# Prompt attention with pre-split operands, dilated sets scored by residue, and shares applied to the outputs

## The reference

```
def fox_prompt(q, k, v, logf):            # causal, with a learned decay
    c = cumsum(logf)
    s = q @ k.T * scale + c[query] - c[key]
    p = softmax(where(key <= query, s, -inf))
    return p @ v

def dilated_prompt(q, k, v, window, dilation):
    # tokens by residue modulo the dilation, then a causal band of window // dilation
    o, lse = band_attn(to_res(q), to_res(k), to_res(v), window // dilation)

for (w, r) in ((128, 1), (512, 4), (2048, 16)):   # each with q, k, v of its own
    o, lse = dilated_prompt(q, k, v, w, r)
a = softmax([lse_1, lse_2, lse_3])                 # merge_groups
o_dil = sum(a_g * o_g)                             # = one softmax over all three key sets
```

## Time and profile before

| | us |
|---|---|
| median of 3 runs (1779.42 to 1780.15) | 1779.7 |
| span of the profiled execution | 1779.2 |
| PE busy in it | 1710.8 |
| DVE busy | 1086.7 |
| ACT busy | 956.5 |
| POOL busy | 868.4 |
| prompt attention, from the first DMA of its block to the first matmul of the next | 1070.2 to 1256.0 |

### The profile page before, as it was taken

One profiled execution on the slowest core, in us unless ns is written; L12 is line 12 of the kernel. 1 busy time (PEld: TensorE's weight loads), 2 busy tenths in 40 slices (PEclk: granted clock), 3 DMA queues, 4 the chain that ended last, 5 costly groups with the idle time before them and its releaser, 6 DMA issues. The chain is left out here.

```text
span 1779.2 us, 32332 instructions
## 1 busy us (share of the span) xinstructions
PE 1710.8 (96%) x10749; PEld 1529.3 (86%) x10749; DVE 1086.7 (61%) x2480; ACT 956.5 (54%) x1649; POOL 868.4 (49%) x496
## 2 busy tenths in 40 slices
PE   6999999999889999999999977898999999999998
PEld 5888888899889999899899956888998989899897
DVE  6747556422388888888888877888444514234251
ACT  5444344432368887888888877988314313122230
POOL 1615233300338878778788747775233433333332
PEclk9999999999999999999999998999999999999999
DMA  7386585645889999999999976320645566666662
GB/s 238 106 290 216 202 300 183 207 132 137 253 308 365 344 351 350 353 347 336 355 360 349 316 232 163 91 73 25 215 146 214 235 259 236 259 236 260 236 259 77
DMA packets 191563, 427.76 MB, mean 240 GB/s; under 512 B 22761, under 2 KB 86122, under 8 KB 190002
## 3 DMA queue, kind: packets, MB, share of 16 engines
q1 hardware_dynamic: 187474, 415.29, 66.8%
q10 hardware_dynamic: 2560, 8.39, 1.6%
q0 software_dynamic: 1376, 2.10, 0.5%
HBM read 392.36 MB, written 120.64 MB: 288 GB/s over the span
## 5 line engine op out<-in xcount | busy, mean ns | idle before, releaser
L1086 POOL TENSOR_TENSOR vv_lo<-v_raw,vv_hi 128x1024 fp32r<-128x1024 f32 x178 | 401.4, 2261 | 147.9 <-ACT vv_hi L1175 145.7
L1986 POOL TENSOR_TENSOR w_lo<-w_raw,w_hi 128x2048 fp32r<-128x2048 f32 x39 | 180.1, 4619 | 318.4 <-ACT w_hi L2000 318.4
L1167 ACT ACTIVATE kt_hi<-ktp 128x1024 fp32r<-128x1024 f32 (+1 forms) x192 | 186.2, 970 | 94.0 <-PE ktp L1351 93.2
L1191 DVE TENSOR_TENSOR kt_lo<-ktp,kt_hi 128x1024 fp32r<-128x1024 f32 (+1 forms) x192 | 220.9, 1151 | 8.1 <-ACT kt_hi L1167 6.2
L1365 PE MATMUL s_ps<-kt_hi,q_st 128*128 128x256 f32 (+3 forms) x768 | 205.9, 302 | 0.8 <-DVE mx_parts L1241 0.4
L1351 PE MATMUL ktp<-ident,k_raw 128*128 128x128 f32 x1440 | 192.0, 276 | 8.3 <-DVEq L1182 3.8
L1351 PEld LDWEIGHTS ktp<-ident,k_raw 128*128 128x128 f32 x1440 | 168.6, 142 | 32.7 <-issue 5.6
L707 PE MATMUL acc<-w_hi,xn_hi 128*128 128x512 f32 x480 | 192.4, 401 | 2.4 <-POOL w_lo L340 2.4
L1175 ACT ACTIVATE vv_hi<-v_raw 128x1024 fp32r<-128x1024 f32 (+1 forms) x192 | 191.4, 997 | 6.2 <-PE o_ps L1381 5.7
L1365 PE MATMUL s_ps<-kt_lo,q_st 128*128 128x256 f32 (+3 forms) x768 | 191.0, 282 | 0.0
L707 PE MATMUL acc<-w_lo,xn_hi 128*128 128x512 f32 x480 | 187.7, 391 | 0.0
(11 more groups left out here) (244 smaller groups left out, 4139.4 us busy)
## 6 DMA issues: line engine op xcount, KB each, us to landing
k_raw<-in_cache_fox_k SPq DMA_DIRECT2D x256, 256.0 KB, 4.9
v_raw<-in_cache_fox_v SPq DMA_DIRECT2D x256, 256.0 KB, 4.6
out_win_kv_sample<-in_cache_win_kv SPq DMA_DIRECT2D x32, 2040.0 KB, 9.5
w_raw<-in_w_in SPq DMA_DIRECT2D x32, 1024.0 KB, 5.9
k_raw<-in_cache_win_kv SPq DMA_DIRECT2D x40, 512.0 KB, 9.5
v_raw<-in_cache_win_kv SPq DMA_DIRECT2D x40, 512.0 KB, 8.6
w_raw<-in_w_up SPq DMA_DIRECT2D x16, 1024.0 KB, 5.3
w_raw<-in_w_down SPq DMA_DIRECT2D x16, 1024.0 KB, 5.1
```

What stands on the lines that cost most here:

```text
L1086: gp.tensor_tensor(vv_lo[:, slot, 0:tiles, :], v_raw[:, i % RAW_RING, 0:tiles, :], vv_hi[:, slot, 0:tiles, :].bitcast(F32), ALU.subtract). ...
L1167: act.activation(kt_hi[:, slot, :, 0:n], ktp[:, i % 2, :, 0:n], ACT.Copy).then_inc(k_hi, 1)
L1191: ve.tensor_tensor(kt_lo[:, slot, :, 0:n], ktp[:, i % 2, :, 0:n], kt_hi[:, slot, :, 0:n].bitcast(F32), ALU.subtract).then_inc(k_lo, 1)
L1986: gp.tensor_tensor(w_lo[slot][:], w_raw[:, slot, :], w_hi[slot][:].bitcast(F32), ALU.subtract).then_inc(slab_lo_done, 1)
```

## The change

It does six things.

1. In `project_tokens` DVE makes the low parts of turned q and k (`turned_rows_lo`, 8 a set) and of v (4 a set), and ACT a high part of v (4 a set) beside the copy. High and low are stored whole, three stores a chunk, to `qh_s`, `ql_s`, `kh_s`, `kl_s`, `vh_s`, `vl_s`. The loops over sets on ACT and DVE become two loops, for sets 0 and 1, and for sets 2 and 3, whose turned columns are laid by residue modulo 4.
2. `attend_prompt` no longer splits anything. POOL issues the loads of the split operands, 2 for a pair's keys, 2 for a head's queries, 8 for a pair's values. Those of the first pair (with two of zeros, in place of `memset`) are issued inside `attend_sample`, after its last keys are scored (`first_pair`); SP issues masks and bias there.
3. Sets 2 and 3 are scored per residue modulo 4: 4 units of two tiles a head (`SPREAD`), which replace 20 tiles. Set 1 (`NEAR`, 7 tiles) and set 0 (`FAR`, 10 tiles) stay. A head has 25 tiles in 7 steps, with three output banks.
4. Each unit of each kind has its own minimum of the negated scores and its own sum: 12 exponentials a head. Probabilities are not normalised.
5. The shares that scale the outputs are worked out per head: NEAR's minima and sums go through DRAM to the residue layout (SP, `send_near`, `take_near`), DVE, POOL and ACT compute shares with small operations, SP stores them and `far`'s inverses and loads all three by broadcast (`send_far`, `send_shares`, `take_shares`).
6. POOL scales and adds the outputs of each pair (`scale`, 4 operations of 128x512). Outputs are evicted by ACT (`copy_spread`) and DVE (`copy_near`, `copy_far`).

```diff
@@ project_tokens, scalar and vector @@
+                if t == Q_TILES:
+                    act.activation(y_t[:, t, :], tp[:, slot, :], ACT.Copy).then_inc(yt_done, 1)
+                else:
+                    act.activation(token_cols(y_hi, t, by_residue), turned_cols(tp[:, slot, :], by_residue), ACT.Copy).then_inc(yt_done, 1)
+                            if t < Q_TILES:
+                                act.activation(v_hi[:, t, :], acc[:, t, :], ACT.Copy).then_inc(vhi_done, 1)
+            def turned_rows_lo(s, c, t, by_residue):
+                slot, at = (5 * c + t) % 2, 10 * s + 5 * c + t
+                ve.wait_ge(yt_done, at + 3)
+                ve.tensor_tensor(token_cols(y_lo, t, by_residue), turned_cols(tp[:, slot, :], by_residue),
+                                 token_cols(y_hi, t, by_residue).bitcast(F32), ALU.subtract).then_inc(ylo_done, 1)
@@ attend_sample, gpsimd @@
+            def first_pair(b, i):
+                if b < DEC_BATCH - 1 or i < LAST:
+                    return
+                done(gp, s_done, group_index(b, LAST))
+                hold(gp)
+                load_keys_of(gp, a, ahead, 0)
+                load_queries(gp, a, ahead, 0, 0)
+                gp.dma_start(ahead["q"][64:128, :, 0].rearrange("p c s n -> p c (s n)"), a["c_zero"].bitcast(F32R)).then_inc(ahead["zeroed"], 16)
...
+            straight(DEC_BATCH, PER_BATCH, (0, per_batch), (EXP_BEHIND, values_lo), (5, first_pair))
@@ attend_prompt @@
+SPREAD, NEAR, FAR = 0, 1, 2
+GROUPS = ((SPREAD, (0, 1)), (SPREAD, (2, 3)), (NEAR, (2, 3)), (NEAR, (0, 1)), (FAR, (3,)), (FAR, (2,)), (FAR, (0, 1)))
+S_BANKS, T_BANKS = 3, 2
@@ sync @@
+            def send_near(h, i):
+                if i == 0:
+                    sp.wait_ge(exp_done, STEPS * h + 4)
+                    sp.dma_start(a["stat_s"][h].rearrange("c (q p) -> p (c q)", p=P), stat[:, h % 2, NEAR].rearrange("p c q -> p (c q)"), allow_slow_non_contiguous=True).then_inc(near_sent, 16)
...
+            straight(HEADS, STEPS, (6, send_near), (7, take_near), (8, bias_ahead),
+                     (10, send_far), (12, send_shares), (13, take_shares))
@@ gpsimd @@
+            load_values(0)
+            gp.wait_ge(masks_in, 16)
...
+            straight(HEADS, STEPS, (0, mask_diagonals), (0, keys_ahead), (7, queries_ahead), (7, values_ahead), (9, gaps), (10, weights), (11, divide), (15, scale))
@@ scalar @@
+            straight(HEADS, STEPS, (EXP_P_BEHIND, exponentials), (TURN_BEHIND, turns_hi), (10, gap_exponentials), (10, copy_spread),
+                     (TURN_BEHIND + 1, split_lead))
@@ vector @@
+            def least_of_both(h, i):
+                if i == 0:
+                    ve.wait_ge(near_in, 16 * (h + 1))
...
+            straight(HEADS, STEPS, (KEEP_BEHIND, keep), (LOW_BEHIND, turns_lo), (9, invert_far), (9, least_of_both), (11, invert_whole), (12, copy_near), (14, copy_far))
             ve.wait_ge(lead_w, 1)
             ve.tensor_tensor(w0_lo[:], w_raw[:, 0], w0_hi[:].bitcast(F32), ALU.subtract)
@@ tensor: score @@
+                    if kind == SPREAD:
+                        lots = [(s, slice(n * P, (n + 1) * P), slice(cols.start + j * P, cols.start + (j + 1) * P)) for j, (s, _) in enumerate(unit_tiles(kind, n))]
+                    else:
+                        s = 0 if kind == FAR else 1
+                        lots = [(s, slice(unit_tiles(kind, n)[0][1] * P, (n + 1) * P), cols)]
+                    for s, keys, out in lots:
+                        for m, (q, part) in enumerate(((q_hi, 0), (q_lo, 0), (q_hi, 1))):
+                            last = pe.matmul(s_ps[:, at % S_BANKS, out], q[:, h % 2, s, n * P:(n + 1) * P], k[p % 2][:, part, s, keys], start=(m == 0), stop=(m == 2))
```

More of the change, by code:

```diff
@@ new lines, in mask_diagonals @@
+            def mask_diagonals(h, i):
+                if i:
+                    return
+                tiles = bias[:, h % 2, :].rearrange("p (t n) -> p t n", n=P)
+                causal = masks[:, 0:P].unsqueeze(1).to_broadcast([P, 2, P])
+                gp.wait_ge(bias_in[h % 2], 16 * (h // 2 + 1))
+                for part in (slice(0, 3, 2), slice(5, 10, 4)):
+                    last = gp.tensor_tensor(tiles[:, part], tiles[:, part], causal, ALU.add)
+                last.then_inc(diag_done, 1)
```

823 lines of the change are left out of this document (421 added, 402 removed).

## The result

The changed kernel takes 1875.3 us, median of 4 runs (1868.6 to 1883.1), against 1779.9 for the kernel before on the same chip: ratio 1.054 (95% interval 1.051 to 1.057). It is slower, and the prediction, 1767 and at most 1797, was wrong. The profiled execution is the longest of the four: its span is 1881.2 us, 102.0 over that of before, where the medians differ by 95.4.

A forecast was written before the change was run, and what follows sets the result against it. PE was taken to bound the prompt loop. Stage 136 + 8.5 + 3 + 15 = 162.5 against 185.8 (-23.3), projection +1.5, end of decode +6, clock +3: -12.8, forecast 1767 us, range 1742 to 1797.

The forecast's parts named there:

- The round trip of NEAR's numbers: Prompt loop: NEAR's exchange through DRAM takes 9 us, and four steps and one bank allow 12 before DVE needs it.
- The rival: Prompt loop: if NEAR's trip takes 15 us, every head loses 3 and the time is 1791; chance 0.07.
- The loop's traffic: Prompt loop: no cost was given to its loads; the DMA share of 0.26 was read from the kernel before.
- The loop, PE: Prompt loop: PE bounds it at 17.0 us a head, 136 for eight, -34.6, with 1.8 a head kept idle.
- The end of decode: End of decode: 5.6 MB more to fetch push back value loads or first scores, +6 us (0 to 18).
- The projection: Projection: DVE's low parts partly fall into its waits, +1.5 us (0 to 11); larger stores stay hidden.
- POOL's issues at 1.0 us: End of decode and prompt stage: each POOL load issue costs 1.0 us, between 0.6 and 4.0; eight take 8 us.
- that rival: Prompt loop and decode: POOL's issues make ACT wait, deciding at about 1.3 us each; 1814 at 2 us; chance 0.17.
- The 18 us by the rule on the shared port: End of decode: eight POOL issues, each waiting for a DVE split of up to 2.3 us, take 18; sum 1777.
- The ends of the stage: Prompt stage: start losses 8.5 us, pipeline drain 3, exposed exchange of the last head 15 (7 to 20).
- The next stage's clock: Last stage: PE idles before it and begins it at the lower clock, +3 us (0 to 7).
- The lower end of the range: Whole kernel: 1742 us, the cheap ends (1752) with half of the loop's idle time gone.

The follow-up runs named there:

- the probes: Kernel before, with SP in the prompt stage storing 4 KB and loading it back, in 4-byte then 32-byte pieces, four times each; 1792.3 us (single run).
- the run with later users: Changed kernel with minimum of both, gaps, weights, division and scaling five steps later and a third statistics buffer; 1876.0 us, ratio 1.052 to the kernel before.
- the run with local numbers and low parts once: Changed kernel without NEAR's trip through DRAM, low parts of q fetched for the first pair only, of k and v for the first two; 1807.2 us.
- the run with small bias: Changed kernel with 32-byte NEAR stores, vn ahead, memset zeros, v's stores behind slabs, later exchange users, and bias fetched as 4 tiles, not 10; 1799.0 us.
- the run with the 32-byte store: Changed kernel storing NEAR's numbers in 32-byte pieces and fetching them by four loads in 4-byte pieces; 1834.1 us, ratio 1.030 to the kernel before.
- vn first: Changed kernel with POOL's first-pair loads issued 12 steps later, behind the two vn loads; 1862.2 us, ratio 1.046 to the kernel before.
- loads early: Changed kernel with 32-byte NEAR stores, memset zeros, v's stores behind slabs, later exchange users, first-pair loads 11 steps earlier than in vn first; 1825.5 us.

## Why the prediction was wrong

- **The round trip of NEAR's numbers (9 us, 12 allowed): the step that failed first.** The store was priced at 5 from a transfer of 512 pieces of 256 bytes, bounds 2.8 and 10; in the probes it takes 10.2 to 12.1 at a DMA share of 0.30 to 0.50, above its own upper bound. The nearest row had pieces 64 times as long, and it was a load where the term is a store. The load was priced at 3 and takes 9.0 beside the loop's traffic (1.6 to 2.6 in the probes, in 32-byte rows). The rival had the mechanism and too small a price: its 1791 at 15 us a trip adds 24 us, and taking the trip away gave back 53, 5.8 us a head at trips of 18 to 25. The sentence beside it, one descriptor for each element, was the rule that spoke against the change, and its chance of 0.07 was too low for a transfer that no row showed. It also left out SP's list: by the run with later users the trip costs the same when DVE doesn't wait for it.
- **The loop's traffic: the step that was missing.** I costed the bytes of the extra loads in the projection and at the end of decode and not in the loop, and took the share of 0.26 of the kernel before for the one after. The loop's share became 1.18; a third of the operands' traffic is worth 2.0 to 2.7 us a head. The stage before moved some 15 MB; it is now 30.
- **The loop, PE (17.0 a head): not what bound it, and met in sum when it was.** With the trip gone and a third of the operands left out it measures 17.0, and the stage 164.7 against 162.5. In part that is luck: PE is idle 1.1 us a head there, not the 1.8 that were kept, and the granted clock is 0.90, where the rows for the prices had 0.99.
- **The end of decode (+6): mis-sized, +38.** "inside the same 6 us delay, not on top" named POOL's issues and not what is queued behind them on the same DMA queue: vn. PE waits 32 us for it. With the order set right 21 us come back, and the bytes hold the rest: 195 to 240 GB/s while POOL's loads are in the queues, not 315. With order and zeros set right, a smaller bias and v's stores behind the slabs, the first score comes at 1078.2, 6 us later than before. That this is the forecast's +6 is a coincidence: two memsets that the forecast didn't have end just ahead of it.
- **The projection (+1.5): mis-sized, +8.3**, inside its bound of 11, by another mechanism: not DVE's room but SP's list.
- **POOL's issues at 1.0 us and that rival: false.** They take 0.60 to 0.80. The 18 us by the rule on the shared port, with its sum of 1777, did not show either, and the passage leaves out a condition: the Trainium skill ("SBUF — State Buffer", section "SBUF: two separate sides") has that lock for DVE operations in a 2-port mode, and for those with two inputs, as these splits are, only against a GpSimd operation that reads SBUF.
- **The ends of the stage: mis-sized by 8.** The forecast leaves 29 us for the start and the end around the 133.6 between first and last score. From the last score to `finish` alone it is 36.9, and 31.0 in the run with local numbers and low parts once. PE's last wait is 13.3 of them, close to the 15 forecast. **The next stage's clock (+3):** 1.0.
- The lower end of the range is 3 us off by its own terms: 1752 less half of the loop's idle time (7 us) is 1745, not 1742. Nothing hangs on it.

An estimate of what is in the change: the front of the run with small bias (first score 1078.2), the stage of the run with local numbers and low parts once (164.7) and `finish` (524.2) make 1767. That is the forecast's number by a coincidence of its parts, for a kernel whose exchange of NEAR's numbers is free and whose operands are a third fewer; the computation as written can't have it. What stays open: 2.4 us in decode's body, what FAR's 4-byte stores cost, operands loaded as float32, and how the whole computation would run with an exchange that isn't made by DMA; none of these was tried.

## What to carry to other kernels

Work that is saved on the engines by storing operands twice as large has to be paid in the queues of every stage that fetches them: recompute the traffic of the stage, don't read it off the kernel before. A high DMA share alone doesn't tell that bandwidth is the limit: take the suspected wait away and see whether the share rises. A transfer's price goes by the length of its pieces and by its direction, and a row of a load with pieces 64 times as long doesn't bound a store; a round trip through DRAM inside a loop also has to be followed on the list of the engine that issues it, or moving its consumer gains nothing. For each DMA that is moved ahead on a queue, name the next one on it that somebody needs at once.

## What the runs showed of the hardware

- A store of 4 KB to DRAM in 4-byte pieces takes 10.2 to 12.1 us at a DMA share of 0.30 to 0.50, in 32-byte pieces 1.4 to 2.3. Reading 4-byte pieces didn't show such a price: in the run with the 32-byte store such loads land in 4.9 us.
- The same 4.2 MB: 1280 packets and 7.9% of the DMA engines' 178 us in float32 on POOL's queue, 8448 packets and 13.2% as fp32r on POOL's queue, some 8400 packets and 8.8% in float32 on SP's.
- POOL issued loads of 256 KB to 1 MB in 0.60 to 0.80 us each, also the eight in decode (1043.8 to 1049.0), beside which three of DVE's splits of 1.2 to 1.8 us ran; no wait for them showed.
- A small load issued by POOL lands behind the large ones ahead of it on the queue: 96 KB behind 6 MB took 43.7 us, behind 4 MB 26.6, and 5.1 ahead of them.
- After decode's last product the next block began 2 to 3 us after the later of two things: the last landing of loads in flight (1095.7, then 1097.7 with vn first) and the end of POOL's last operation (1095.6, then 1098.4 with loads early).
